# MLA heads in pairs on row and column tiles, two thirds of the first condition summed on VectorE, w_out begun before the last pair is finished

## The reference, cut to what matters

```
m  = silu(c) @ w_mod + b_mod                      # 1024 -> 6*1024
sh1, sc1, g1, sh2, sc2, g2 = split(m, 6)          # only sh1, sc1 are needed before the heads
csh1, csc1 = first two pieces of silu(c_ctx) @ w_mod + b_mod
hx = rms_norm(x)*(1+sc1)+sh1;  hc = rms_norm(ctx)*(1+csc1)+csh1
px = hx @ w_in;  pc = hc @ w_in                   # 256 Fourier, 384 q, 256 kv, 64 k_rope columns
q  = rms_norm(q_lat) @ w_q_up                     # 6 heads of 128 (nope) + 64 (rope)
kv = rms_norm(kv_lat) @ w_kv_up                   # 6 heads of 128 (k) + 128 (v), for x and ctx: 512 keys
q_rope, k_rope = rotate(...)                      # k_rope is one for all heads
att = softmax([q, q_rope] @ [k, k_rope].T * 192**-0.5) @ v
x = x + g1 * rms_norm(concat(att, fourier(px)) @ w_out)
```

## Time and profile before

| | us |
|---|---|
| time of three runs, median (lowest, highest) | 2670.73 (2668.48, 2672.01) |
| the profiled execution: its time | 2665.1 |
| its span in the profile | 2663.4 |
| px begins, px ends (L781) | 47.01, about 74 |
| first matmul of w_out (L954), first beyond it (L154) | 208.59, 236.13 |
| mean granted clock of TensorE | 0.987 |

### The profile page before, as it was taken

How to read it: one execution, slowest core, us unless ns; L and a number is a source line. 1 busy time by engine, 2 the same in 40 slices (tenths; PEclk the granted TensorE clock), 3 DMA queues, 4 the chain that set the end, 5 groups by cost and what they waited for, 6 DMA issues and landing times. The chain is left out here.

```text
span 2663.4 us, 34311 instructions
## 1 busy us (share of the span) xinstructions
PE 2527.2 (95%) x13319; PEld 1563.9 (59%) x13320; DVE 1051.3 (39%) x2208; ACT 370.1 (14%) x751; POOL 43.0 (2%) x64
## 2 busy tenths in 40 slices
PE   6998999999999999988999999999999999999998
PEld 3445333333333333335888868877886878676786
DVE  1143122112211211122385249746896543354434
ACT  2122111111111111112022210002001100232001
POOL 0000000000000000000000000000010000000000
PEclk8999999999999999999999999999999999999999
DMA  8603999999999699997743458754997644113452
GB/s 338 245 31 129 422 428 424 429 428 429 428 429 428 254 426 427 428 428 282 280 139 121 184 197 330 268 192 166 353 371 273 249 144 156 70 66 132 142 172 96
DMA packets 188024, 728.33 MB, mean 273 GB/s; under 512 B 9758, under 2 KB 103292, under 8 KB 159156
## 3 DMA queue, kind: packets, MB, share of 16 engines
q1 hardware_dynamic: 168324, 651.29, 62.6%
q0 software_dynamic: 19632, 76.09, 7.2%
HBM read 726.30 MB, written 1.05 MB: 273 GB/s over the span
## 5 line engine op out<-in xcount | busy, mean ns | idle before, releaser
L1507 PE MATMUL bank<-experts_raw,experts_xs 128*64 128x512 f32 x2112 | 483.1, 605 | 54.5 <-DMA experts_raw<-in_w_gate 49.3
L1507 PEld LDWEIGHTS bank<-experts_raw,experts_xs 128*64 128x64 f32 x2112 | 149.2, 139 | 356.5 <-issue 278.9
L2422 PE MATMUL bank<-big,ffn_actT 128*128 128x512 f32 x704 | 309.1, 592 | 0.0
L1660 DVE COPY tiled_spread<-bank 128x256 f32<-128x256 f32 x33 | 14.0, 425 | 709.8 <-PE bank L1540 709.8
L1507 PE MATMUL bank<-experts_raw,tiled_act_s 128*64 128x512 f32 x1056 | 237.8, 592 | 1.4 <-DVE tiled_act_s L1699 1.4
L1825 PE MATMUL bank<-hT,ring 128*128 128x256 f32 x1024 | 223.6, 380 | 1.1 <-ACT hT L419 1.1
L2422 PEld LDWEIGHTS bank<-big,ffn_actT 128*128 128x128 f32 x704 | 130.6, 190 | 148.3 <-issue 148.3
L1825 PEld LDWEIGHTS bank<-hT,ring 128*128 128x128 f32 x1024 | 194.9, 191 | 29.9 <-issue 3.5
L2297 PEld LDWEIGHTS bank<-hT,big 128*128 128x128 f32 x1408 | 163.5, 192 | 20.0 <-issue 20.0
L2297 PE MATMUL bank<-hT,big 128*128 128x128 f32 x1408 | 164.6, 275 | 2.0 <-DVE hT L459 2.0
L1507 PEld LDWEIGHTS bank<-experts_raw,tiled_act_s 128*64 128x64 f32 x1056 | 76.7, 137 | 151.0 <-issue 151.0
(11 more groups left out here) (482 smaller groups left out, 2678.2 us busy)
## 6 DMA issues: line engine op xcount, KB each, us to landing
experts_raw<-in_w_gate SPq DMA_DIRECT2D x64, 2048.0 KB, 13.9
experts_raw<-in_w_up SPq DMA_DIRECT2D x64, 2048.0 KB, 19.1
experts_raw<-in_w_down SPq DMA_DIRECT2D x64, 2048.0 KB, 10.5
big<-in_ffn_w_gu SPq DMA_DIRECT2D x88, 1024.0 KB, 9.5
ring<-in_mod_w POOLq DMA_DIRECT2D x30, 2048.0 KB, 10.9
big<-in_ffn_w_down SPq DMA_DIRECT2D x44, 1024.0 KB, 4.9
ring<-in_w_in SPq DMA_DIRECT2D x16, 2048.0 KB, 8.8
mla_wm<-in_w_mod SPq DMA_DIRECT2D x24, 1024.0 KB, 6.9
```

What stands on the lines that cost most here:

```text
L1507: last = nc.tensor.matmul(bank[b][h * HALF:(h + 1) * HALF, :], stationary(kt), raw[p][:, k, h * C:(h + 1) * C], start=kt == 0, stop=kt == ...
L1660: vec.tensor_copy(spread[:], bank[X][:, 0:SEQ]).then_inc(spread_ready, 1)
L2422: last = nc.tensor.matmul(bank[b][:], actT[:, s, f, t * P:(t + 1) * P], wd[:, s, f, n * 512:(n + 1) * 512], start=start and f == 0, stop=s ...
```

## The change

- **Pairs of heads.** Heads are worked on two at a time (three pairs). `kr` and `rot` get 128 rows: rows 0 to 63 for the first head of a pair, 64 to 127 for the second; k_rope is held twice. k_rope's products for x and ctx alternate between two column tiles of 64, as do the rope projections of the two heads. The rotation partner is one matmul of 128 rows with a block-diagonal table. The rope products of the two heads stand next to each other on two row tiles of 64, into different banks.
- **Condition.** Chunks 8 to 23 no longer go to TensorE. VectorE adds each, multiplied by silu(c) per row, onto `sums` (128 x 2048 for each of two pairs of pieces; row 0 starts from the bias, the others from zero). After the last, `conditions()` sums over rows on TensorE: 16 matmuls that move one column of ones, and 4 of 512 columns with 128x128 ones as weights. Two b_mod rows more are loaded at the end of SP's list in `mla_norm`, four fewer in its middle; GpSimd zeroes `sums` (128 x 4096).
- **Order.** The values v are made between the first two pairs. w_out's first two outputs are begun with the k-tiles of pairs 0 and 1 and of the Fourier part, before and after `values(2)`; the late k-tiles 4 and 5 follow.
- Buffers are shared differently: `prob[0]` lies in the buffer of ctx's columns, `probT` in that of the latents; `qT` and `qr` are single. The normalisation of the latents is done in two steps (four parts of px, then two of pc).

```diff
+        def add_chunk(dve, c):
+            pair, j = c // KT - 1, c % KT
+            dve.wait_ge(*wm_in[c % RING].next(dve))
...
+            if j:
+                dve.wait_ge(*wm_used[(c - 1) % RING].own())
+            nc.vector.scalar_tensor_tensor(sums[:, pair, :], wm[c % RING][:], core.cpad[:, j, 0:1], sums[:, pair, :],
+                                           ALU.mult, ALU.add).then_inc(*wm_used[c % RING].up())
...
-                for pair in range(3):
-                    for which in range(2):
-                        sp.dma_start(brows[which:P:32, pair, :], ins["b_mod"][4 * pair:4 * pair + 4, :])\
-                            .then_inc(*brows_in.up())
+                for which in range(2):
+                    sp.dma_start(brows[which:P:32, :], ins["b_mod"][0:4, :]).then_inc(*brows_in.up())
...
+                for pair in range(2):
+                    sp.dma_start(sums[0:1, pair, :], ins["b_mod"][4 * pair + 4:4 * pair + 8, :]
+                                 .rearrange("(o a) n -> o (a n)", o=1)).then_inc(*sums_in.up())
...
+                nc.gpsimd.memset(sums[:], 0.0)
...
                 for c in range(KT + RING, 3 * KT):
-                    if (c - RING) % KT == KT - 1:
-                        sp.wait_ge(*core.filled[mod_bank[(c - RING) // KT]].ahead(1))
-                    else:
-                        sp.wait_ge(*wm_used[c % RING].next(sp))
+                    sp.wait_ge(*wm_used[c % RING].next(sp))
                     load_chunk(sp, c)
...
+                for k in range(KT):
+                    for s, src in enumerate((core.hT, ctx_hT)):
+                        last = nc.tensor.matmul(bank[5][s * ROPE:(s + 1) * ROPE, 0:SEQ], w_in[:, k, W_IN1 - ROPE:W_IN1],
+                                                src[:, k, :], start=k == 0, stop=k == KT - 1)
...
+                def project(p):
+                    keys(2 * p)
+                    core.claim(pe, 1)
+                    for i in range(2):
+                        for k in range(QT):
+                            last = nc.tensor.matmul(bank[1][:, i * SEQ:(i + 1) * SEQ], wq_heads[:, k, 2 * p + i, 0:NOPE],
+                                                    qlT[:, k, :], start=k == 0, stop=k == QT - 1)
+                    fill(last, 1, ("nope", p))
+                    core.claim(pe, 2)
                     for k in range(QT):
+                        for i in range(2):
+                            last = nc.tensor.matmul(bank[2][i * ROPE:(i + 1) * ROPE, 0:SEQ],
+                                                    wq_heads[:, k, 2 * p + i, NOPE:], qlT[:, k, :],
+                                                    start=k == 0, stop=k == QT - 1)
+                    fill(last, 2, ("rope", p))
+                    keys(2 * p + 1)
...
                     for t in range(TT):
+                        mine = slice(t * P, (t + 1) * P)
+                        for i in range(2):
+                            b = 3 + 2 * i + t
+                            core.claim(pe, b)
+                            nc.tensor.matmul(bank[b][:], qT[:, i, mine], kT[i][:], start=True, stop=False)
+                        for i in range(2):
+                            b, rows = 3 + 2 * i + t, slice(i * ROPE, (i + 1) * ROPE)
+                            fill(nc.tensor.matmul(bank[b][:], qr[rows, mine], kr[rows, :], start=False, stop=True),
+                                 b, ("scores", p, i, t))
...
+                def conditions():
+                    for s in range(RING):
+                        pe.wait_ge(*wm_used[s].ahead(sum(c % RING == s and c != KT - 1 for c in range(3 * KT))))
+                    core.claim(pe, 2)
+                    for i, (pair, a) in enumerate(((0, PIECE), (1, 0))):
+                        for j in range(KT):
+                            last = nc.tensor.matmul(bank[2][:, i * KT + j:i * KT + j + 1],
+                                                    sums[:, pair, a + j * P:a + (j + 1) * P], core.ones[:, 0:1],
+                                                    start=True, stop=True)
+                    fill(last, 2, "columns")
...
                 project(0)
+                make_v(0)
                 turn(0)
...
+                make_v(1)
+                scores(0)
                 project(1)
+                make_v(2)
                 turn(1)
+                make_v(3)
+                turn_prob(0)
                 scores(1)
+                project(2)
...
+                values(0)
+                turn(2)
+                turn_prob(1)
+                scores(2)
+                values(1)
+                conditions()
+                turn_prob(2)
...
                 pe.wait_ge(*w_out_in.next(pe))
+                early, late = (0, 1, 2, 3, 6, 7), (4, 5)
+                out(0, early)
+                values(2)
+                out(1, early)
+                taken(pe, ("out", 2))
+                out(0, late)
+                out(1, late)
+                out(2, early + late)
+                out(3, early + late)
```

More of the change, by code:

```diff
@@ new lines, in project, with turn, make_v @@
+                    fill(last, 2, ("rope", p))
+                    keys(2 * p + 1)
+                def turn(p):
+                    taken(pe, ("rope", p))
+                    core.claim(pe, 2)
+                    fill(nc.tensor.matmul(bank[2][:, SEQ:], table("turn1"), rot[:, 0, :], start=True, stop=True),
+                         2, ("turned", p))
+                def make_v(t):
+                    for n, b in enumerate((7, 0)):
+                        core.claim(pe, b)
+                        for k in range(KVT):
+                            heads = wkv[:, k, :].rearrange("p (h c) -> p h c", c=NOPE + VDIM)
+                            last = nc.tensor.matmul(bank[b][:, 0:3 * VDIM], kvT[:, k, t * P:(t + 1) * P],
+                                                    heads[:, 3 * n:3 * n + 3, NOPE:], start=k == 0, stop=k == KVT - 1)
+                        fill(last, b, ("v", t, n))
@@ L925, in _ @@
+                taken(pe, ("qlT", 2), ("qlT", 3), ("kvT", 0), ("kvT", 1))
                 project(0)
-                core.copied(pe, 7)
-                core.claim(pe, 7)
-                turn_rows(pe, 2, 7)
+                make_v(0)
                 turn(0)
+                taken(pe, "ff")
+                core.claim(pe, 4)
+                for g in range(2):
+                    last = nc.tensor.matmul(bank[4][:, g * SEQ:(g + 1) * SEQ], wf[:, g, :], ff[:, g, :],
+                                            start=True, stop=True)
@@ new lines, in _ @@
+                take_v(1)
+                chunks(1)
+                maxima(0)
+                chunks(1)
+                finish(0)
+                take_q(1)
+                take_v(2)
+                rotate(1)
+                take_v(3)
+                chunks(2)
+                maxima(1)
+                chunks(1)
+                finish(1)
+                take_q(2)
+                take_out(0)
+                rotate(2)
+                chunks(2)
+                maxima(2)
+                take_out(1)
@@ new lines, in root @@
+                def root(first, end):
+                    act.wait_ge(*lat_mean.next(act))
+                    run(stat[:, 12 + first:12 + end], stat[:, 6 + first:6 + end], ACT.Sqrt).then_inc(*lat_root.up())
+                for t in range(TT):
+                    src = ready(act, ("px", t, 1))
+                    run(px[:, t, 448:], src[:, 0:448], ACT.Copy).then_inc(*free(("px", t, 1)))
+                taken(act, *[("px", t, n) for t in range(TT) for n in range(2)])
+                squares(0, 4)
@@ L1116, in _ @@
+                src = ready(act, "kr")
+                for rows in range(2):
+                    for half in range(2):
+                        op = run(kr[rows * ROPE:(rows + 1) * ROPE, half * SEQ:(half + 1) * SEQ],
+                                 src[half * ROPE:(half + 1) * ROPE, 0:SEQ], ACT.Copy)
+                op.then_inc(*free("kr"))
+                root(0, 4)
+                taken(act, "pc")
+                squares(4, 6)
+                root(4, 6)
                 gain = core.column("norm_kv_lat", 0, KVT)
@@ L1168, in _ @@
+                for i in range(2):
+                    for n in range(2):
+                        src = ready(act, ("gate", i, n))
+                        run(core.gate1[:, i, n * 512:(n + 1) * 512], src[:], ACT.Copy).then_inc(*free(("gate", i, n)))
+                take_turned(2)
                 for b in (3, 4, 5, 6):
```

562 lines of the change are left out of this document (238 added, 324 removed).

## The result

The changed kernel takes 2630.9 us (median of four runs, 2622.1 to 2634.4) against 2669.6 us beside it; the ratio is 0.9851 with the interval 0.9822 to 0.988. The forecast was 2637.8 us with the range 2630 to 2647, so the time lies at the lower edge of it. Over all executions of this study the kernel before has a mean of 2668.3 us (48 executions, standard deviation 4.6) and the changed one 2626.1 us (10 executions, 4.9): 42 us less, where 33 were forecast.

A forecast was written before the change was run, and what follows sets the result against it. The stage was taken as bound by TensorE. Condition -13.0, pairs of heads -17.3, waits and clock -2.6 sum to -32.9 us; from a median of 2670.7 us that gives 2637.8 us, range 2630 to 2647 (8 in 10).

The forecast's parts named there:

- chunks: 16 condition chunks leave TensorE's list in this stage, at 0.925 us each: -14.8 us.
- turns of rows: Two of the three groups of 8 transposes for the condition go from TensorE: -1.0 us.
- gates: Four gate halves on TensorE keep their passes but use all 128 rows: -0.8 us allowing for overlap.
- columns: 16 one-column matmuls (32 instructions) added on TensorE to sum the condition over rows: +3.6 us.
- Row tiles and column tiles at 1.92 times: Pairs of 64-row or 64-column products on TensorE run side by side, 1.92 times as fast; all pair terms: -17.3 us.
- rivals 2 and 3: Paired products on TensorE overlap only in part (+3.4 us, 2641 us, chance 0.06) or not at all (+12.9 us, 2651 us, 0.06).
- VectorE hides the chunks, 17 us free: From 94 to 163 us VectorE has 69 us for 51.5 us of work, ten chunks at 2.35 us included; added 0.
- the tight place: VectorE's first copy of take_q(2) is ready 0.6 us before TensorE wants its bank for values(0); cost 0 to 2 us.
- Ahead of px, cost 0: Bias loads moved in SP's list and a longer memset before px were costed at 0, covered by SP's idle time.
- The slower cases: VectorE's ten chunks between heads make the kernel slower (chance 0.03), or the gain is swallowed behind the stage (2670 us, 0.02).
- Waits and clock: TensorE's waits in the stage: -5.3 us gone, +1.2 and +1.5 new; clock -1.7 and +1.7; sum -2.6 us.
- the likeliest case: The forecast's own case, chance 0.62, 2633 to 2643 us: allowances for the one-column price, VectorE's closest deadline and the pairs' pace.

The follow-up runs named there:

- the loads moved and put back: Four short bias loads moved to the end of SP's list in the kernel before: 2665.8 us; put back mid-list, into a spare buffer, in the changed kernel: 2625.4 us.
- 26 dummies: Either kernel with 26 instead of 18 matmuls ahead of px whose result nobody reads: before 2663.2 us, ratio 0.9988; changed 2625.0 us, ratio 0.9831.

## Why the prediction was right and where it was not

**The list of TensorE, term by term.** Each group's time from its start to the next group's, without waits, summed over the stage, in the second profile of before and the first of the changed kernel:

| term | forecast | measured | of it low clock |
|---|---|---|---|
| chunks | -14.8 | -15.9 | -0.9 |
| turns of rows | -1.0 | -1.1 | |
| gates | -0.8 | +1.9 | +2.6 |
| columns | +3.6 | +4.4 | +0.8 |
| k_rope | -3.4 | -3.4 | |
| rope projections | -4.3 | -4.3 | |
| rotation partner | -2.1 | -2.3 | |
| scores | -7.5 | -7.5 | |
| waits (the forecast with clock, -1.7 + 1.7) | -2.6 | -2.8 | |
| Fourier products | | -1.2 | -0.8 |
| values v, values, nope | | -1.5 | |
| the rest | | +0.3 | |
| sum | -32.9 | -33.4 | +1.7 |

So the stage came out as forecast, 0.5 us off, but not because every part was right. At full clock (the measured column less its last) each term of the forecast is right within 0.3 us. Beside them stand two amounts that the forecast did not have and that offset each other, which is luck: 1.7 us more lost to the clock, and 2.2 us more work gone (35.1 at full clock for 32.9), of which 1.5 us lies in products that the change only regrouped. "Row tiles and column tiles at 1.92 times" was right: rivals 2 and 3 (overlap in part, or none) are out by k_rope's 3.61 us, by the 2.87 us of a score block, where the sum had 2.96, and by the kernel with the rope products apart. The ratios in the Trainium skill, "TensorE: Matmul & The Clock Gate", Part 3 ("Measured speedup vs the span model"), are for three tiles and more; the 1.57 for two that the prediction estimated from them does not hold here: 7.05/3.61 is 1.95. "VectorE hides the chunks, 17 us free" was nearly right (15 us), and so was the tight place (0.8 us of play for 0.6). "Ahead of px, cost 0" was right, as the kernels with the loads moved and put back show. The slower cases did not come: nothing behind the stage took the gain, the rest being 2428.7 us before and 2428.0 after in the mean of three profiles each.

**The step that failed** is the clock in "Waits and clock", and with it the range. The prediction set -1.7 for the wait at the Fourier product against +1.7 for the columns and had 0 for the clock everywhere else. First, +1.7 was too small: in the three profiles of the changed kernel the clock stood at 1.2 GHz for 6.8 us at the columns and behind them, not 3.4, and that cost 3.4 us. The place was right: in all nine profiles of the changed kernel and its variants with 18 dummies the clock fell 2.3 to 4.0 us after the columns began, for 3.4 or 6.8 us. But the place is not all: in the one profile of each kernel with 26 dummies, the kernel before kept its wait of 2.2 us and had no low clock in the stage, and the changed kernel kept its columns and had none. Second, the clock counts outside the stage too, where the sum had 0. Grouped by the mean granted clock of an execution (the values that both kernels have):

| mean granted clock | before, mean us (executions) | changed, mean us (executions) | difference |
|---|---|---|---|
| 0.986 | 2671.3 (10) | 2634.4 (1) | 36.9 |
| 0.987 | 2667.4 (15) | 2630.7 (2) | 36.7 |
| 0.988 | 2663.4 (7) | 2626.5 (2) | 36.9 |
| 0.990 | 2661.2 (2) | 2622.6 (4) | 38.6 |

At the same clock the change is worth 37 us: 35.1 us of work, and some 2 us that I can't place. The other 5 us of the 42 go with the mean clock itself, 0.9868 before and 0.9887 after, at 2.4 us for each 0.001 (a straight line through the executions of both kernels and of the timed variants). Of that, px shows 2.0 us (26.8 us before, 24.8 after, in the mean of three profiles), while the stage takes back 1.7. So 4 to 5 us of clock lie elsewhere, and where stays open: the profiled executions don't show them. Three of each kernel were profiled, of 2664.5 and 2628.7 us in the mean. They differ by 35.8 us and not by 42, which is the stage's 33.4, px's 2.0 and little else, and in them the time at 1.2 GHz behind w_out is alike (40 to 49 us before, 37 to 49 after). Whether it belongs to the change or to which executions were drawn is not settled either: the third profiles showed that px's clock varies within each kernel.

Of the miss of 6.9 us against the first median, then, 0.5 us is the stage, about 2.0 px's clock, and 2.4 the start: the 2670.7 us of three runs were that much over the mean of 48. The remaining 2 us are within the spread of four runs. The range of the likeliest case (2633 to 2643) had terms for edits only and none for this spread, though the first four runs of the changed kernel alone lie 12 us apart.

## What to carry to other kernels

When a change acts in one stage, compare the stage at full clock (its length less half of the time at 1.2 GHz in it): here it repeated within 0.1 us, while the whole time spread over 14 us and more. Work taken from the bounding engine pays in full only if the list is closed up behind it: where 12 chunks were cut without that, half of their 9.9 us came back as waits, and in the one execution profiled the clock took the rest and more. Before moving work to an idle engine, walk both lists and find the free time between the deadlines, not the busy share: from 68.6 to 166.3 us VectorE is idle for 36 of 97.7 us in the changed kernel, but only 15 us more could be hidden in the order given.

## What was unexpected of the hardware

- Two products on two column tiles, issued one tile after the other, overlap at the seam: three passes of 256 started before the first tile was done, and k_rope took 6.25 us, where 32 passes at 0.216 us from start to start would be 6.9.
- With 12 chunks cut from the kernel before, the clock stood at 1.2 GHz for 13.7 us though TensorE was busy 13.78 of 14 us. In this window 16 instructions ran instead of 39 because of it: two passes of 512 took 2.0 us from start to start instead of 1.05. The same scores and gate halves, behind the same wait of 1.0 us, ran at full clock in the kernel before, where the 31 us ahead had no gap (here TensorE was busy 29.3 of them). What brought the clock down is not shown.
- One-column matmuls cost 0.11 us a pass at full clock, in a row and between passes of 512 alike.
- In the first profile of the changed kernel TensorE waited 4.4 us for the first w_in load of the second block; in its third profile it did not, and the rest was 12.7 us shorter (2434.8 and 2422.1 us). Of the other 8 us 6 are clock: it stood at 1.2 GHz for 49.4 and 36.9 us there.
